# One sum of squares for two norms between the blocks of a fused fp32 transformer kernel

## The chip, the cores and the metric

The kernel runs on one core of one Trainium2 chip. The metric is the device time of one execution in microseconds (us), the median of the runs.

## What is computed

A sequence of 256 tokens of width 1024 passes through two blocks, all in fp32. The first block has two layers (mixed attention, cross attention to a memory, a gated MLP) and ends with a norm, the second block has two layers (retention, short convolution, each with a SwiGLU) and begins with another norm. Between the blocks the reference does this:

```python
def rms_norm(x, g):                        # end of the first block: g = norm_final
    y = x * lax.rsqrt(jnp.mean(x * x, axis=-1, keepdims=True) + EPS)
    return y * g

def rms_norm_2(x, gain=None):              # start of the second: gain = norm_mix_2[0]
    y = x * lax.rsqrt(jnp.mean(x * x, axis=-1, keepdims=True) + EPS)
    return y * gain

ax = modulate(rms_norm_2(hx, norm_mix[i]), sh1, sc1)     # hx = first block's output
ac = modulate(rms_norm_2(hc, norm_mix[i]), csh1, csc1)   # hc = the context
```

With x the residual stream and g the first norm's gain, the first norm gives y = x g r1, where r1 = 1 / sqrt(mean(x^2) + eps). The second norm's factor is r2 = 1 / sqrt(mean(y^2) + eps). The input of the retention is x g r1 r2 times the second gain, then scaled and shifted. Multiplied out, r1 r2 = 1 / sqrt(mean(x^2 g^2) + eps mean(x^2) + eps^2) = 1 / sqrt(mean(x^2 (g^2 + eps)) + eps^2). The residual stream of the second block is y, which needs r1 alone.

## The kernel before

Activations lie feature-first: 8 blocks (`kb`) of 128 features by 256 tokens. TensorE multiplies fp32 weights in split form: ScalarE copies each streamed piece of 128x1024 from the ring buffer to a high half `WH` (line 489), VectorE subtracts to get the low half `WL` (line 1067), and TensorE does high by high, high by low and low by high (`rows` or `FH`/`FL` hold the activations' halves). Two buffers each for `WH` and `WL` alternate. A piece can be split when TensorE is done with the piece two places before.

The weights stream through a ring of 8 pieces of 512 KB, issued by SyncE in one fixed order. SyncE issues a piece when VectorE has used the one 7 places before, and reports a piece as `loaded` only when it has issued the one 5 places behind it. So ScalarE can read a piece only when VectorE has used the piece three places ahead. Mixed into the stream are `ada` pieces, the modulation weights, which VectorE alone reduces (`ada_piece`, line 1084).

Each engine has its own program, in one fixed order; the order on an engine is that of the Python code of its block, and semaphores tie the engines together. A stage has steps of two pieces. Its loop takes `after(step)`, a function called behind every step, and so side work is set between pieces. The stages around the change are:

- `down` of layer 1 (k0 + 7, or K - 1): 11 steps, two pieces and two `ada` pieces a step. Its side work is the context's norm: ScalarE squares the context (steps 0 and 1), TensorE sums (`summed`), ScalarE copies the sums (`side_sums`), TensorE totals them (`total`), ScalarE takes the root (`raw_root`, behind a load of the table for square roots), VectorE takes the reciprocal (`root(rstd_m)`, line 1200), `scaled` (line 1206) on VectorE, `high` on ScalarE (line 621) and `low` (line 1233) on VectorE make the halves of the context's rows. Then the residual (line 1093) adds the sums in four banks to `x`.
- The gap between the blocks: squares of x, their sum, root, reciprocal (r1); squares of x times gain, their sum, times r1 squared, root, reciprocal (r2). Then eight times `scaled`, `high`, `low`, one for each block of features. `scr` has eight blocks of 128x256: `scr1` is its first half, for squares, `scr2` the second, for scaled blocks.
- `rq` (K), 4 steps: queries. `first_step` waits for each block's high and low. VectorE's side work at step 0 multiplies x by gain and r1 (line 1598); the rotations (`sine`, `turned_by`) begin at step 2.
- `rk` (K + 1), 4 steps with products over own and context rows, 512 columns wide, and two `ada` pieces a step; then `rg` (K + 2).

`turn_over` issues fill matmuls on zeros. `summed`, `gate_logits` and others sum into four groups of 32 rows of a bank, each with ones of 32 columns, to be totalled by a further matmul.

Of the kernel before, what the change touches and what calls it, by code (L numbers as in the profile page):

```python
# [7 lines left out]
S = 256  # L8
D = 1024
KB = D // 128  # L10
# [8 lines left out]
EPS = 1e-6  # L19
# [82 lines left out]
V_FINAL1 = _take(KB)  # L102
# [100 lines left out]
def transformer(nc, xT_d, memT_d, ctxT_d, cond_d, stream_d, vecs_d, const_d, rope1_d, rope2_d, decay_d,  # L203
                gw_d, w1_d, w2_d, out_d):
    F32, F32R, BF16 = mybir.dt.float32, mybir.dt.float32r, mybir.dt.bfloat16
    ALU, ACT, AX = mybir.AluOpType, mybir.ActivationFunctionType, mybir.AxisListType

    ctx = ExitStack()
    with ctx:  # L209
        def sb(name, shape, dt=F32):  # L210
            return ctx.enter_context(nc.sbuf_tensor(name, shape, dt))

        def sem(name):
            return ctx.enter_context(nc.semaphore(name))
# [6 lines left out]
        x = sb("x", [128, KB, S])  # L221
        both = sb("rows", [128, 2 * KB, 2, S + 2], F32R)
        AHs, ALs = both[:, 0:KB, :, :], both[:, KB:2 * KB, :, :]
        AH, AL = AHs[:, :, :, 0:S], ALs[:, :, :, 0:S]
        scr = sb("scr", [128, 8, S])
        scr1, scr2 = scr[:, 0:4, :], scr[:, 4:8, :]
        rms = sb("rms", [128, S])
# [33 lines left out]
        mod = sb("mod", [128, DEPTH * 48])  # L261
        modc = sb("modc", [128, 2 * KB])
        gs = sb("gs", [128, 6, KB])

        ARENA = 80 * 1024
        arena_at = nc.sbuf_base
# [2 lines left out]
        def at(name, shape, kb, dt=F32):  # L269
# [51 lines left out]
        misc = ob[1]  # L321
# [38 lines left out]
        in_cond, mod_ready, ret_sc, ret_w, ret_o, ret_g, ret_sq, ret_ms, ret_rms, ret_t, ret_h, ret_l = (  # L360
            sem(n) for n in ("in_cond", "mod_ready", "ret_sc", "ret_w", "ret_o", "ret_g", "ret_sq", "ret_ms", "ret_rms", "ret_t", "ret_h", "ret_l"))
        y_ready, out_done, ret_v = sem("y_ready"), sem("out_done"), sem("ret_v")
        both_ready = sem("both_ready")
        taken_ready = sem("taken_ready")
        tok_mm, tok_high, tok_low, ret_sum = (sem(n) for n in ("tok_mm", "tok_high", "tok_low", "ret_sum"))
        sum_ready, ms_done, gl_ready, gate_sum, conv_ready = (
            sem(n) for n in ("sum_ready", "ms_done", "gl_ready", "gate_sum", "conv_ready"))

# [113 lines left out]
        def _(act):  # L482
# [82 lines left out]
            def squares(blocks):  # L565

                def go():
                    act.preload_act_table(ACT.Sqrt)
                    for kb in range(KB):
                        x_is(n["x"] + kb // blocks + 1)  # L570
                        square(x, n["norm"], kb)
                return go
# [133 lines left out]
            for i in range(DEPTH):  # L706
# [172 lines left out]
                if i == 0:  # L879
                    raw_norm(k0 + 7, vecs[:, V_MIX + KB:V_MIX + 2 * KB], 0, 2, evac=last_rows)  # L880
                else:
                    def context(step):

                        if step in (0, 1):
                            act.wait_ge(in_ctx, 16)
                            for kb in range(4 * step, 4 * step + 4):
                                A(scr[:, kb, :], ctxT[:, kb, :], ACT.Square).then_inc(sq_ready, 1)
                        if step == 3:
                            side_sums()
                        if step == 5:  # L890
                            act.preload_act_table(ACT.Sqrt)
                            raw_root()
                        if step in (7, 9):
                            act.wait_ge(mod_ready, 1)
                            for kb in range(2 * step - 14, 2 * step - 10):
                                high(n["scaled"], kb, shift=modc[:, 0:8], sel=1)
                    weights(k0 + 7, last_rows, banks=False, tail=squares(2), after=context)
                    n["split"] += 1
                    n["scaled"] += 1
                    n["x"] += 4  # L900
# [22 lines left out]
                    n["x"] += 8  # L923


            def gained_square(kb):
                act.wait_ge(sq_used, 8 * n["norm"] + kb + 5)
                A(scr1[:, kb % 4, :], x[:, kb, :], ACT.Square, scale=vecs[:, V_FINAL1 + kb:V_FINAL1 + kb + 1]).then_inc(sq_ready, 1)
            for kb in range(4):
                gained_square(kb)  # L930
            act.wait_ge(sq_used, 8 * n["norm"] + 8)
            A(rms[:], misc[:, 0:S], ACT.Sqrt, bias=eps, scale=1.0 / D).then_inc(rms_ready, 1)
            for kb in range(4, KB):
                gained_square(kb)
            n["norm"] += 1
            act.wait_ge(both_ready, 1)
            A(rms[:], prod[:], ACT.Sqrt, bias=eps, scale=1.0 / D).then_inc(rms_ready, 1)
            n["norm"] += 1
            act.wait_ge(mod_ready, 1)
            for kb in range(KB):  # L940
                high(n["scaled"], kb, shift=mod_of(0, 0))
            n["split"] += 1
# [14 lines left out]
            def queries(i, s):  # L957
                A(Q2[:, i * 2 + s, :], proj[s][:, 0:S], ACT.Copy).then_inc(bank_free[s], 1)
                if s == 0 and i:
                    swap(i - 1)  # L960
            weights(K, queries, after=lambda step: None)

            def keys(i, s):
                A(K2[:, i * 2 + s, :], proj[s][:], ACT.Copy, scale=256 ** -0.5).then_inc(bank_free[s], 1)
# [95 lines left out]
        def _(dve):  # L1060
# [137 lines left out]
            def root(dst=None):  # L1198
                dve.wait_ge(rms_ready, n["norm"] + 1)
                chain.link(V.reciprocal((dst or rstd)[:], rms[:]))  # L1200
                n["norm"] += 1

            def scaled(m, src, gain, kb, by):
                if kb >= 4:
                    dve.wait_ge(nl_ready, 8 * m + kb - 3)
                V.scalar_tensor_tensor(out=scr2[:, kb % 4, :], in0=src[:, kb, :], scalar=gain[:, kb:kb + 1], in1=by[:],
                                       op0=ALU.mult, op1=ALU.mult).then_inc(t_ready, 1)
# [315 lines left out]
            def context_low(*blocks):  # L1523
                for kb in blocks:
                    low(n["split"], kb, sel=1, shift=modc[:, 0:8])

            def context(step):

                if step == 4:
                    chain.link(V.tensor_tensor(modc[:], modc[:], vecs[:, V_ADAB:V_ADAB + 16], ALU.add))  # L1530
                    modulations(0)
                    chain.link(V.tensor_tensor(gs[:, 5, :], gs[:, 0, :], vecs[:, V_FINAL1:V_FINAL1 + KB], ALU.mult))
                if step == 6:
                    root(rstd_m)
                    dve.wait_ge(in_ctx, 16)
                if step == 8:
                    context_low(0, 1, 2, 3)
                if step in (6, 8):
                    for kb in range(2 * step - 12, 2 * step - 8):
                        scaled(n["split"], ctxT, gs[:, 4, :], kb, rstd_m)  # L1540
            weights(K - 1, last_rows, into_x=True, after=context, ahead=lambda: context_low(4, 5, 6, 7))
            n["split"] += 1
            root()
            chain.link(V.tensor_tensor(rstd_m[:], rstd[:], rstd[:], ALU.mult))
            dve.wait_ge(sq_used, 8 * n["norm"] + 8)
            V.tensor_tensor(prod[:], ob[0][:, 0:S], rstd_m[:], ALU.mult).then_inc(both_ready, 1)
            root(rstd_m)
            chain.link(V.tensor_tensor(rstd_m[:], rstd_m[:], rstd[:], ALU.mult))
            for kb in range(KB):
                scaled(n["split"], x, gs[:, 5, :], kb, rstd_m)  # L1550
                if kb:
                    low(n["split"], kb - 1, shift=mod_of(0, 0))
            low(n["split"], KB - 1, shift=mod_of(0, 0))
# [39 lines left out]
            def turns(step):  # L1593

                if step == 0:
                    dve.wait_ge(in_rope2, 16)
                    for kb in range(KB):
                        V.scalar_tensor_tensor(out=x[:, kb, :], in0=x[:, kb, :], scalar=vecs[:, V_FINAL1 + kb:V_FINAL1 + kb + 1], in1=rstd[:],
                                               op0=ALU.mult, op1=ALU.mult).then_inc(x_ready, 1)
                    n["x"] += KB  # L1600
                if 3 <= step <= 10:
                    turned_by(step - 3)
                if 2 <= step <= 9:
                    sine(step - 2)
# [210 lines left out]
        def _(pe):  # L1815
# [3 lines left out]
            def mm(out, lhsT, rhs, start, stop):  # L1819
                return T.matmul(out, lhsT, rhs, start=start, stop=stop, skip_group_check=True)  # L1820

            def turn_over(count, bank=ob[0]):

                for _ in range(count):
                    mm(bank[:], still[:, 0:128], still[:], True, True)
# [7 lines left out]
            def sum_squares(kb, bank=misc):  # L1833
                pe.wait_ge(sq_ready, 8 * n["norm"] + kb + 1)
                mm(bank[:, 0:S], ones, scr1[:, kb % 4, :], kb == 0, kb == KB - 1).then_inc(sq_used, 1)
# [15 lines left out]
            def total():  # L1851

                pe.wait_ge(sum_ready, n["raw"] + 1)
                mm(misc[:, S:2 * S], ones, rms[:], True, True).then_inc(ms_done, 1)
                n["raw"] += 1
# [473 lines left out]
            def second_ffn(k, gated):  # L2329
                make(k, XS(AHs), XS(ALs), S + 2, raw=True)  # L2330
                add_gated(k + 1, gated - FB, FB)
            for bank in (misc, ob[0]):
                for kb in range(KB):
                    sum_squares(kb, bank)
                n["norm"] += 1
            n["split"] += 2
            turn_over(18, acc[3])

            def ret_scores(h):
                if h == 0:  # L2340
# [47 lines left out]
                pe.wait_ge(ret_qs, h + 1)  # L2388
                mm(proj[0][:, S:2 * S], ones, rms[:], True, True).then_inc(ret_ms, 1)

            make(K, X(AH), X(AL), fresh=True, after=lambda step: None)
            make(K + 1, XM(AH), XM(AL), 2 * S)
            make(K + 2, X(AH), X(AL), after=tokens)

# [156 lines left out]
```

## Time and profile before

| | before |
|---|---|
| median of 3 runs | 1561.16 us (1561.01 to 1561.27) |
| the profiled execution's own time | 1560.88 us |
| its span, first to last instruction | 1559.2 us |
| TensorE busy | 1530.3 us, 98% |
| VectorE busy | 1147.6 us, 74% |
| ScalarE busy | 865.2 us, 55% |
| GpSimd busy | 110.6 us, 7% |
| mean DMA rate | 191 GB/s |

The profile gives the time of every instruction in microseconds from the start of the span. PE is TensorE, PEld its weight loads, DVE VectorE, ACT ScalarE, POOL GpSimd, SP SyncE. A line number is that of the kernel, and it can be a helper's: every matmul has L1820. An fp32 matmul of the kind that isn't split appears as two records. The ends of matmuls are modelled and overlap the next start.

### The profile page before, as it was taken

How to read it: one execution, taken by the hardware profiler on the slowest of the kernel's cores; microseconds unless marked ns; L12 is line 12 of the kernel's file. 1: busy time of each engine (PE TensorE's matmuls, PEld its weight loads, DVE VectorE, ACT ScalarE, POOL GpSimd, SP SyncE). 2: the span in 40 equal slices, each digit the busy share in tenths (PEclk: the TensorE clock that was granted, in tenths of full speed). 3: DMA queues.
4: the chain of work that ended last, by engine and by line, in shares of the span. 5: the costliest groups of instructions: out<-in, count | busy, mean ns of one | idle time of the engine just before them, and what ended most of it. 6: DMA issues, size and time to landing. Idle time of an engine off the chain costs nothing. (4 is left out here: it accounts for less than half of the span.)

```text
span 1559.2 us, 35029 instructions
## 1 busy us (share of the span) xinstructions
PE 1530.3 (98%) x12576; PEld 1447.8 (93%) x12576; DVE 1147.6 (74%) x1707; ACT 865.2 (55%) x1444; POOL 110.6 (7%) x91
## 2 busy tenths in 40 slices
PE   9999999999999999999999999999999999999998
PEld 7977799999996879999888999999999999999997
DVE  6874788888876578888965556798887478676644
ACT  4665787754457578775543433346554365555533
POOL 2200012210300002220011000000000000000000
PEclk9999999999999999999999999999999999999999
DMA  9521455568641345558847534497888555455551
GB/s 373 198 82 54 150 166 185 188 213 272 244 163 55 122 156 187 183 189 303 292 136 224 167 126 171 148 344 257 278 272 265 185 166 178 160 189 186 179 188 41
DMA packets 84247, 297.62 MB, mean 191 GB/s; under 512 B 9664, under 2 KB 12480, under 8 KB 83392
## 3 DMA queue, kind: packets, MB, share of 16 engines
q1 hardware_dynamic: 78768, 283.24, 53.9%
q10 hardware_dynamic: 5392, 13.18, 2.5%
q8 instruction: 59, 0.97, 0.3%
q14 instruction: 28, 0.23, 0.0%
HBM read 291.40 MB, written 1.05 MB: 188 GB/s over the span
## 5 line engine op out<-in xcount | busy, mean ns | idle before, releaser
L489 ACT ACTIVATE WH<-ring 128x1024 fp32r<-128x1024 f32 (+1 forms) x418 | 441.3, 1058 | 502.5 <-PE projs L1820 256.5
L1067 DVE TENSOR_TENSOR WL<-ring,WH 128x1024 fp32r<-128x1024 f32 x427 | 524.4, 1229 | 224.4 <-ACT WH L489 222.8
L1820 PE MATMUL projs<-rows,WH 128*128 128x256 f32 (+2 forms) x3504 | 488.5, 288 | 1.8 <-ACT rows L621 0.7
L1820 PEld LDWEIGHTS projs<-rows,WH 128*128 128x128 f32 x3504 | 449.1, 189 | 15.1 <-issue 2.7
L1820 PE MATMUL projs<-rows,WL 128*128 128x256 f32 (+2 forms) x1808 | 260.6, 286 | 0.0
L1820 PEld LDWEIGHTS projs<-rows,WL 128*128 128x128 f32 x1808 | 235.6, 189 | 6.0 <-DVE WL L1067 2.1
L1820 PE MATMUL accs<-rows,WH 128*128 128x256 f32 (+2 forms) x1312 | 189.9, 283 | 3.7 <-DVE rows L1289 1.9
L1820 PE MATMUL accs<-FH,WH 128*128 128x256 f32 (+1 forms) x768 | 190.9, 284 | 1.2 <-DVE WL L1067 1.2
L1820 PE MATMUL accs<-FL,WH 128*128 128x256 f32 (+1 forms) x768 | 189.8, 281 | 0.0
L1820 PEld LDWEIGHTS accs<-rows,WH 128*128 128x128 f32 x1312 | 172.4, 189 | 7.3 <-DVE rows L1289 3.1
L1820 PEld LDWEIGHTS accs<-FH,WH 128*128 128x128 f32 x768 | 144.3, 188 | 3.1 <-issue 2.9
L1820 PEld LDWEIGHTS accs<-FL,WH 128*128 128x128 f32 x768 | 144.8, 189 | 0.0
L1084 DVE SCALAR_TENSOR_TENSOR ring<-ring,crow 128x1024 f32<-128x1024 f32 (+1 forms) x96 | 117.0, 1219 | 2.3
L1820 PE MATMUL accs<-FH,WL 128*128 128x256 f32 (+1 forms) x768 | 113.6, 282 | 0.9 <-DVE WL L1067 0.9
L1820 PE MATMUL accs<-rows,WL 128*128 128x256 f32 (+2 forms) x720 | 107.2, 283 | 0.0
L1820 PEld LDWEIGHTS accs<-FH,WL 128*128 128x128 f32 x768 | 101.1, 188 | 1.3 <-DVE WL L1067 1.3
L1820 PEld LDWEIGHTS accs<-rows,WL 128*128 128x128 f32 x720 | 94.7, 189 | 1.3 <-DVE WL L1067 0.7
L1795 POOL TENSOR_TENSOR FL<-prod,FH 128x256 f32 x44 | 62.5, 1422 | 330.5 <-ACT FH L553 330.5
L1462 DVE TENSOR_TENSOR cv<-cv,taps 128x510 f32<-128x510 f32 x44 | 30.4, 691 | 37.8 <-ACT cv L848 37.8
L848 ACT ACTIVATE cv<-mk,vecs 128x256 f32<-128x256 f32 x88 | 47.5, 588 | 0.0
L666 ACT ACTIVATE scr<-accs,nmax 128x256 f32<-128x256 f32 (+1 forms) x96 | 39.7, 435 | 8.7 <-DVE nmax L1261 8.7
L553 ACT ACTIVATE FH<-prod 128x256 fp32r<-128x256 f32 (+1 forms) x88 | 36.2, 411 | 9.6 <-DVE prod L1564 4.7
(284 smaller groups left out, 1727.4 us busy)
## 6 DMA issues: line engine op xcount, KB each, us to landing
ring<-in_stream SPq DMA_DIRECT2D x532, 512.0 KB, 4.2
W1v<-in_w ACTq DMA_DIRECT2D x2, 1024.0 KB, 7.8
W1k<-in_w ACTq DMA_DIRECT2D x2, 1024.0 KB, 11.6
D<-in_decay ACTq DMA_DIRECT2D x4, 512.0 KB, 5.3
x<-in_xT SPq DMA_DIRECT2D x2, 512.0 KB, 5.6
memT<-in_memT SPq DMA_DIRECT2D x1, 1024.0 KB, 10.0
mq<-P ACTq DMA_DIRECT2D x8, 128.0 KB, 6.1
ctxT<-in_ctxT ACTq DMA_DIRECT2D x1, 1024.0 KB, 8.2
```

What stands on the lines that cost most here:

```text
L489: A(WH[:, s, :], ring[:, r % RING, :], ACT.Copy).then_inc(wh_ready, 1)
L553: A(FH[:, step, :], prod[:], ACT.Copy).then_inc(fh_ready, 1)
L666: ins = A(prob[:, g, c:c + w], score[:, g, c:c + w], ACT.Exp, bias=nmax[:, u % 2, g, qt:qt + 1], accum_out=sums[:, u % 2, g, qt:qt + 1])
L848: ins = A(cv[:, s, :], us[:, s, :], ACT.Identity, bias=vecs[:, cb + j:cb + j + 1], scale=vecs[:, cw + 4 * FB + j:cw + 4 * FB + j + 1])
L1067: V.tensor_tensor(WL[:, s, :], ring[:, r % RING, :], WH[:, s, :].bitcast(F32), ALU.subtract).then_inc(consumed, 1)
L1084: V.scalar_tensor_tensor(out=piece, in0=piece, scalar=1.0, in1=crow[:], op0=ALU.mult, op1=ALU.mult, accum_out=mod[:, bass.ds(j, 1)]).then_ ...
L1462: chain.link(V.tensor_tensor(cv[:, :, 1:S], cv[:, :, 1:S], taps[:, :, 0:S - 1], ALU.add))
L1795: G.tensor_tensor(FL[:, bass.ds(step, 1), :].squeeze(1), prod[:], FH[:, bass.ds(step, 1), :].squeeze(1).bitcast(F32), ALU.subtract).then_i ...
L1820: return T.matmul(out, lhsT, rhs, start=start, stop=stop, skip_group_check=True)
```

## The change

The squares of x are taken once, into all eight blocks of `scr` (`block_squares`), as the tail of `down`. TensorE sums them twice: with columns of g^2 + eps (`g2eps`) as the stationary operand, broadcast to 128 columns, which gives the sum of x^2 (g^2 + eps) over all features; and with ones of 32 columns into four groups of rows of `ob[0]`. The first sum, with eps^2 as the bias, gives the product of both factors by one root and one reciprocal, and `scaled` uses it. The second sum is copied by ScalarE after step 0 of `rq`, totalled by TensorE after step 1, its root taken after step 2, its reciprocal after step 3, and x is multiplied by gain and r1 after step 0 of `rk`. The fill matmuls in the gap go from 18 to 8. Three small VectorE operations make `g2eps` and eps^2. In `down`, the context's side work from ScalarE's `side_sums` on moves one step earlier; TensorE's part of it stays where it is, and so do VectorE's last four lows. The load of the table for square roots ahead of the squares is gone.

```diff
@@ tiles, semaphores
+        g2eps = sb("g2eps", [128, KB])
+        eps2 = sb("eps2", [128, KB])
-        both_ready = sem("both_ready")
+        own_mm = sem("own_mm")
@@ ScalarE, down of layer 1
-                        if step == 3:
+                        if step == 2:
                             side_sums()
-                        if step == 5:
+                        if step == 4:
                             act.preload_act_table(ACT.Sqrt)
                             raw_root()
-                        if step in (7, 9):
+                        if step in (6, 8):
                             act.wait_ge(mod_ready, 1)
-                            for kb in range(2 * step - 14, 2 * step - 10):
+                            for kb in range(2 * step - 12, 2 * step - 8):
                                 high(n["scaled"], kb, shift=modc[:, 0:8], sel=1)
-                    weights(k0 + 7, last_rows, banks=False, tail=squares(2), after=context)
+                    def block_squares():
+                        for kb in range(KB):
+                            x_is(n["x"] + kb // 2 + 1)
+                            A(scr[:, kb, :], x[:, kb, :], ACT.Square).then_inc(sq_ready, 1)
+                    weights(k0 + 7, last_rows, banks=False, tail=block_squares, after=context)
@@ ScalarE, between the blocks
-            def gained_square(kb):
-                act.wait_ge(sq_used, 8 * n["norm"] + kb + 5)
-                A(scr1[:, kb % 4, :], x[:, kb, :], ACT.Square, scale=vecs[:, V_FINAL1 + kb:V_FINAL1 + kb + 1]).then_inc(sq_ready, 1)
-            for kb in range(4):
-                gained_square(kb)
+            act.wait_ge(mod_ready, 1)
             act.wait_ge(sq_used, 8 * n["norm"] + 8)
-            A(rms[:], misc[:, 0:S], ACT.Sqrt, bias=eps, scale=1.0 / D).then_inc(rms_ready, 1)
-            for kb in range(4, KB):
-                gained_square(kb)
+            A(rms[:], misc[:, 0:S], ACT.Sqrt, bias=eps2[:, 0:1], scale=1.0 / D).then_inc(rms_ready, 1)
             n["norm"] += 1
-            act.wait_ge(both_ready, 1)
-            A(rms[:], prod[:], ACT.Sqrt, bias=eps, scale=1.0 / D).then_inc(rms_ready, 1)
-            n["norm"] += 1
-            act.wait_ge(mod_ready, 1)
...
-            weights(K, queries, after=lambda step: None)
+            def own_norm(step):
+                if step == 0:
+                    act.wait_ge(own_mm, 1)
+                    A(rms[:], ob[0][:, 0:S], ACT.Copy).then_inc(sum_ready, 1)
+                if step == 2:
+                    raw_root()
+            weights(K, queries, after=own_norm)
@@ VectorE, down of layer 1
-                if step == 4:
+                if step == 3:
+                    first_gain = vecs[:, V_FINAL1:V_FINAL1 + KB]
+                    chain.link(V.tensor_tensor(g2eps[:], first_gain, first_gain, ALU.mult))
+                    chain.link(V.tensor_scalar(g2eps[:], g2eps[:], EPS, None, ALU.add))
+                    chain.link(V.tensor_tensor(eps2[:, 0:1], eps, eps, ALU.mult))
...
-                if step == 6:
+                if step == 5:
                     root(rstd_m)
                     dve.wait_ge(in_ctx, 16)
-                if step == 8:
+                if step == 7:
                     context_low(0, 1, 2, 3)
-                if step in (6, 8):
-                    for kb in range(2 * step - 12, 2 * step - 8):
+                if step in (5, 7):
+                    for kb in range(2 * step - 10, 2 * step - 6):
                         scaled(n["split"], ctxT, gs[:, 4, :], kb, rstd_m)
-            weights(K - 1, last_rows, into_x=True, after=context, ahead=lambda: context_low(4, 5, 6, 7))
+                if step == 9:
+                    context_low(4, 5, 6, 7)
+            weights(K - 1, last_rows, into_x=True, after=context)
@@ VectorE, between the blocks
             root()
-            chain.link(V.tensor_tensor(rstd_m[:], rstd[:], rstd[:], ALU.mult))
-            dve.wait_ge(sq_used, 8 * n["norm"] + 8)
-            V.tensor_tensor(prod[:], ob[0][:, 0:S], rstd_m[:], ALU.mult).then_inc(both_ready, 1)
-            root(rstd_m)
-            chain.link(V.tensor_tensor(rstd_m[:], rstd_m[:], rstd[:], ALU.mult))
+            dve.wait_ge(own_mm, 1)
             for kb in range(KB):
-                scaled(n["split"], x, gs[:, 5, :], kb, rstd_m)
+                scaled(n["split"], x, gs[:, 5, :], kb, rstd)
@@ VectorE, turns
+                if step == 3:
+                    root(rstd_m)
+                if step == 4:
                     for kb in range(KB):
                         V.scalar_tensor_tensor(out=x[:, kb, :], in0=x[:, kb, :], scalar=vecs[:, V_FINAL1 + kb:V_FINAL1 + kb + 1], in1=rstd_m[:],
@@ TensorE
-            for bank in (misc, ob[0]):
-                for kb in range(KB):
-                    sum_squares(kb, bank)
-                n["norm"] += 1
+            pe.wait_ge(mod_ready, 1)
+            for kb in range(KB):
+                pe.wait_ge(sq_ready, 8 * n["norm"] + kb + 1)
+                mm(misc[:, 0:S], g2eps[:, kb:kb + 1].to_broadcast([128, 128]), scr[:, kb, :], kb == 0, kb == KB - 1).then_inc(sq_used, 1)
+            for kb in range(KB):
+                c = kb % 4
+                ins = mm(ob[0][32 * c:32 * c + 32, 0:S], ones[:, 0:32], scr[:, kb, :], kb < 4, kb >= 4)
+            ins.then_inc(own_mm, 1)
+            n["norm"] += 1
             n["split"] += 2
-            turn_over(18, acc[3])
+            turn_over(8, acc[3])
...
-            make(K, X(AH), X(AL), fresh=True, after=lambda step: None)
+            make(K, X(AH), X(AL), fresh=True, after=lambda step: total() if step == 1 else None)
```

## Rows read from the trace of the kernel before

**Rows 1.** The page, busy us, share of the span, instructions, by engine.

```profile
PE 1530.3 (98%) x12576; PEld 1447.8 (93%) x12576; DVE 1147.6 (74%) x1707; ACT 865.2 (55%) x1444; POOL 110.6 (7%) x91
```

**Rows 2.** TensorE's waits, 736 to 770: us in total, times, longest.

```profile
PE accs L1820 <- DVE WL L1067: 2.1, 3, 1.2
```

**Rows 3.** VectorE's timeline in `down`: start, us, instruction, [idle before <-releaser].

```profile
745.39 1.22 DVE L1067 TENSOR_TENSOR WL<-ring,WH 128x1024 fp32r<-128x1024 f32 x1 [0.51 <-ACT WH L489]
...
747.67 1.75 DVE L1200 RECIPROCAL rstd_m<-rms 128x256 f32<-128x256 f32 x1
...
751.05 1.22 DVE L1067 TENSOR_TENSOR WL<-ring,WH 128x1024 fp32r<-128x1024 f32 x1
...
760.17 1.66 DVE L1233 SCALAR_TENSOR_TENSOR rows<-scr,modc,rows 128x256 fp32r<-128x256 f32 x4
...
767.90 1.67 DVE L1233 SCALAR_TENSOR_TENSOR rows<-scr,modc,rows 128x256 fp32r<-128x256 f32 x4
769.49 2.47 DVE L1093 TENSOR_TENSOR x<-x,accs 128x512 f32<-128x512 f32 x4
```

**Rows 4.** TensorE's timeline in `down`: low passes, and the last piece's start.

```profile
731.20 1.12 PE L1820 MATMUL accs<-FH,WL 128*128 128x256 f32 x8
...
734.50 1.12 PE L1820 MATMUL accs<-FH,WL 128*128 128x256 f32 x8
...
746.02 1.12 PE L1820 MATMUL accs<-FH,WL 128*128 128x256 f32 x8
...
748.90 1.12 PE L1820 MATMUL accs<-FH,WL 128*128 128x256 f32 x8
...
752.32 1.22 PE L1820 MATMUL accs<-FH,WL 128*128 128x256 f32 x8 [0.39 <-DVE WL L1067]
...
766.98 0.36 PE L1820 MATMUL accs<-FH,WH 128*128 128x256 f32 x1 [1.16 <-DVE WL L1067]
```

**Rows 5.** ScalarE's timeline in `down`: the piece behind step 4.

```profile
735.65 1.06 ACT L489 ACTIVATE WH<-ring 128x1024 fp32r<-128x1024 f32 x1 [2.24 <-PE accs L1820]
```

**Rows 6.** TensorE's timeline between the blocks.

```profile
770.67 3.72 PE L1820 MATMUL ob<-scr,const 128*128 128x256 f32 x16 [0.58 <-ACT scr L563]
...
778.36 4.05 PE L1820 MATMUL accs<-still 128*128 128x512 bf16 x18
783.11 6.35 PE L1820 MATMUL projs<-rows,WH 128*128 128x256 f32 x32 [0.70 <-ACT rows L621]
...
791.91 2.12 PE L1820 MATMUL projs<-rows,WH 128*128 128x256 f32 x16 [0.57 <-ACT Q L958]
```

**Rows 7.** VectorE's timeline between the blocks.

```profile
774.15 1.22 DVE L1067 TENSOR_TENSOR WL<-ring,WH 128x1024 fp32r<-128x1024 f32 x1 [0.94 <-ACT WH L489]
776.11 1.75 DVE L1200 RECIPROCAL rstd<-rms 128x256 f32<-128x256 f32 x1 [0.73 <-ACT rms L932]
...
781.88 0.88 DVE L1206 SCALAR_TENSOR_TENSOR scr<-x,gs,rstd_m 128x256 f32<-128x256 f32 x2
```

**Rows 8.** Timeline of the kernel's last norm, TensorE and VectorE.

```profile
1546.67 3.69 PE L1820 MATMUL ob<-scr,const 128*128 128x256 f32 x16 [0.15 <-PE accs L1820]
...
1551.03 1.75 DVE L1200 RECIPROCAL rstd<-rms 128x256 f32<-128x256 f32 x1 [3.41 <-ACT rms L576]
1552.82 3.26 DVE L1241 SCALAR_TENSOR_TENSOR ybuf<-x,vecs,rstd 128x256 f32<-128x256 f32 x8
```

**Rows 9.** TensorE's timeline, eight sums of 32 columns in a later stage.

```profile
1261.69 1.07 PE L1820 MATMUL ob<-scr,const 128*32 128x256 f32 x16
```

**Rows 10.** VectorE's timeline in `rq`: x times gain and rstd.

```profile
793.90 3.25 DVE L1598 SCALAR_TENSOR_TENSOR x<-x,vecs,rstd 128x256 f32<-128x256 f32 x8
```

**Rows 11.** TensorE's timeline, the kernel's first matmuls.

```profile
1.39 7.01 PE L1820 MATMUL ob<-still 128*128 128x512 bf16 x18 [1.39 <-POOL still L1738]
```

**Rows 12.** Windows: stretch, its us, busy us by engine, granted clock, DMA share.

```profile
769.50:783.10 13.60, 12.15 (x55) 7.85 (x55) 10.66 (x15) 8.58 (x21) 0.00 (x0) 1.00 0.42 148
783.10:791.90 8.80, 7.92 (x48) 6.21 (x49) 5.99 (x15) 4.78 (x10) 0.00 (x0) 1.00 0.00 0
```

More of the change, by code:

```diff
@@ L1527, in context @@
             def context(step):
-                if step == 4:
+                if step == 3:
[3 more added lines that the diff above has]
+                    chain.link(V.tensor_tensor(eps2[:, 0:1], eps, eps, ALU.mult))
                     chain.link(V.tensor_tensor(modc[:], modc[:], vecs[:, V_ADAB:V_ADAB + 16], ALU.add))
                     modulations(0)
-                    chain.link(V.tensor_tensor(gs[:, 5, :], gs[:, 0, :], vecs[:, V_FINAL1:V_FINAL1 + KB], ALU.mult))
-                if step == 6:
+                    chain.link(V.tensor_tensor(gs[:, 5, :], gs[:, 0, :], first_gain, ALU.mult))
+                if step == 5:
                     root(rstd_m)
                     dve.wait_ge(in_ctx, 16)
-                if step == 8:
+                if step == 7:
                     context_low(0, 1, 2, 3)
-                if step in (6, 8):
-                    for kb in range(2 * step - 12, 2 * step - 8):
+                if step in (5, 7):
+                    for kb in range(2 * step - 10, 2 * step - 6):
                         scaled(n["split"], ctxT, gs[:, 4, :], kb, rstd_m)
-            weights(K - 1, last_rows, into_x=True, after=context, ahead=lambda: context_low(4, 5, 6, 7))
+                if step == 9:
+                    context_low(4, 5, 6, 7)
+            weights(K - 1, last_rows, into_x=True, after=context)
             n["split"] += 1
             root()
-            chain.link(V.tensor_tensor(rstd_m[:], rstd[:], rstd[:], ALU.mult))
-            dve.wait_ge(sq_used, 8 * n["norm"] + 8)
-            V.tensor_tensor(prod[:], ob[0][:, 0:S], rstd_m[:], ALU.mult).then_inc(both_ready, 1)
-            root(rstd_m)
-            chain.link(V.tensor_tensor(rstd_m[:], rstd_m[:], rstd[:], ALU.mult))
+            dve.wait_ge(own_mm, 1)
             for kb in range(KB):
-                scaled(n["split"], x, gs[:, 5, :], kb, rstd_m)
+                scaled(n["split"], x, gs[:, 5, :], kb, rstd)
                 if kb:
@@ L1596, in turns @@
                     dve.wait_ge(in_rope2, 16)
+                if step == 3:
+                    root(rstd_m)
+                if step == 4:
                     for kb in range(KB):
-                        V.scalar_tensor_tensor(out=x[:, kb, :], in0=x[:, kb, :], scalar=vecs[:, V_FINAL1 + kb:V_FINAL1 + kb + 1], in1=rstd[:],
+                        V.scalar_tensor_tensor(out=x[:, kb, :], in0=x[:, kb, :], scalar=vecs[:, V_FINAL1 + kb:V_FINAL1 + kb + 1], in1=rstd_m[:],
                                                op0=ALU.mult, op1=ALU.mult).then_inc(x_ready, 1)
```

## The prediction

> **What bounds the kernel now.** I read the page first. TensorE is busy for 98% of the span [rows 1], so time can only be won where TensorE waits or does work that can go. Next I read TensorE's waits inside the stage ahead of the change, then the timelines of the three engines around the boundary between the blocks.
>
> In `down` of layer 1, the last stage of the first block, TensorE waits three times for VectorE's low halves `WL`, 2.1 us in all [rows 2]. VectorE's timeline says why: its split `WL` at 745.39 still has 0.51 us of idle before it (so has the one before it), and from 747.67 it never rests until the residual at 769.49 [rows 3]. The context's reciprocal and scalings lie there on top of two splits and two `ada` pieces a step. TensorE's low passes come every 2.88 us, as 748.90 after 746.02, but 752.32 is 3.42 after 748.90, and the last piece starts at 766.98 after 1.16 us of idle [rows 4].
>
> Then comes the gap between the blocks. TensorE starts the first sum of squares at 770.67, the first product of `rq` at 783.11 and its second step at 791.91 [rows 6]. The chain is: first sum (TensorE) to 774.4, ScalarE's root, reciprocal at 776.11, a product of rstd with itself, a product with the second sum, a second root, a second reciprocal, one more product, and the first `scaled` at 781.88 [rows 7]. After that, eight pairs of `scaled` and `low` on VectorE set the pace. The 18 fill matmuls end at 782.4, ahead of the product, so they don't bind [rows 6].
>
> **The change part by part.** All times below are in the clock of the profile before, unless I say "shifted".
>
> *(a) One root and one reciprocal in place of two.* The new chain (sum, root, reciprocal, scaling) is the one that the kernel runs as its last norm, so I price it from there: sum starts 1546.67, reciprocal 1551.03 (4.36 later), first scaling 1552.82 (6.15 later) [rows 8]. From 770.67 this gives the reciprocal at 775.03 and the first `scaled` at 776.82. VectorE must be free: its second split for `rq` ran from 774.15 to 775.37 [rows 7], behind ScalarE's second `WH`, which stands behind the squares. The squares now need no freed buffer (eight buffers instead of four), so they follow the residual, which ends some 2.5 us after 769.49, plus two squares; that is 0.3 to 0.4 us earlier than now. The split then ends at about 775.0, just in time. First `scaled` at 776.84 instead of 781.88: **5.0 us** less; 4.7 if the split isn't earlier. Gone with it are four gained squares and four VectorE products, all inside this difference.
>
> *(b) The first sum has another stationary operand*, a column of `g2eps` broadcast, in place of ones. Same eight fp32 matmuls, 3.72 us [rows 6]. I take zero; the pace of that group is the bound, and a stride can't make a loading of 128 columns shorter.
>
> *(c) The own sums, eight matmuls to four groups of 32 rows.* The same form takes 1.07 us for its 16 records [rows 9]. They end at about 775.3; VectorE waits for them (`own_mm`) before its first `scaled`, which overwrites their input, and would start only at 776.84. Hidden, with 1.5 us to spare. The Trainium skill (TensorEngine Tiling, Key Properties) says that a change of tiling mode drains TensorE, which speaks against inserting these here. With the drain the own sums would end a little later; as they have 1.5 us to spare, the result by that rule is the same unless a drain costs more than this. The 1.07 us group lies between products of full width [rows 9].
>
> *(d) Eight fill matmuls instead of 18.* 18 take 4.05 us [rows 6], so eight take 1.8: 775.3 to 777.1. The first product comes 1.23 us after the first `scaled` (783.11 after 781.88), so at 778.07. Not binding. TensorE idles 0.95 us there, against 0.70 now.
>
> *(e) The pairs* keep their number and form; the stretch from first `scaled` to 791.91 moves as a whole. Its end is ScalarE's `WH` and `Q`, which depend on TensorE alone.
>
> *(f) The first norm's own root.* The total is one more fp32 matmul of full width on TensorE, after step 1 of `rq`, where TensorE is never idle, so it is paid in full. In `down` the same total makes the low passes 731.20 and 734.50 lie 3.30 apart instead of 2.88 [rows 4]: **0.4 us** more. ScalarE's copy and root (under 0.5 us each) lie in its idle time: a piece costs it a `WH` (1.06 us [rows 5]) and a short copy, against 2.8 us or more of TensorE. VectorE's reciprocal, 1.75 us [rows 7], comes after step 3, where VectorE has two splits of 1.2 us a step, and the eight scalings of x, 3.25 us [rows 10], move from step 0 of `rq` to step 0 of `rk`. There a step has 512 columns, and a piece lasts twice as long; a split made late by 3.3 us is for a piece that TensorE begins some 5.6 us later. Zero, both before (the split behind the scalings stalled nothing) and after. Queued behind this ScalarE and VectorE work are only splits and the rotations, whose DMAs have many us.
>
> *(g) The context's steps, each one earlier in `down`.* Three more small VectorE operations at step 3 (0.6 us together, like the five there now) meet no late piece. ScalarE's table load and root after step 4 fall into 2.24 us of idle ahead of the `WH` at 735.65 [rows 5]; TensorE's total, between its low passes 731.20 and 734.50, is done in time. The reciprocal and four scalings, 3.38 us (747.67 to 751.05), now begin at 741.9. The four lows and four scalings, twice 1.6 us from 760.17, come one step earlier too [rows 3]. The last lows stay directly ahead of the residual. VectorE's work is the same; what it gains is the idle in front of its splits of step 6, twice 0.51 us. Followed piece by piece: the root's block ends at 745.3, TensorE waits 0.55 for the low half wanted at 746.02, VectorE catches up to within a piece, the second block makes it wait 0.7 near 758.2, the last piece's low half is ready at 765.7, when TensorE is just through with the one before, and the 1.16 us of idle is gone. The lows end at 768.4, and the residual starts 1.0 to 1.1 us earlier. ScalarE may read a ring entry only when VectorE has used the entry three places ahead; with these times that comes before the need each time. **1.0 us** less, between nothing and 1.2.
>
> Sum: 5.0 + 1.0 - 0.4 = 5.6 us. Behind the gap TensorE waits for nothing that hangs on an absolute time: before the second step of `rq` the ring is full (no DMA runs from 783.1 to 791.9 [rows 12]), and a shorter pause leaves it full. So the gain reaches the end whole. Against the profiled execution's own time of 1560.88 us (span 1559.2) this gives 1555.3; the median of the runs is 0.28 us above that execution, so the forecast is **1555.5 us**.
>
> **The rivals.**
>
> *A. The earlier context steps win nothing.* VectorE is late by a whole block at steps 6 and 8 instead of 7 and 9; if these make ScalarE's `WH` wait for ring entries, VectorE idles later for what it saved. For it: many `WH` here start on a release by the ring. Against: every block is absorbed within two pieces. Time 1555.5 + 1.0 = 1556.5 us.
>
> *B. The own sums become the wait.* If the four row groups don't overlap, eight matmuls take as long as the first sum, 3.7 us instead of 1.1, and end near 777.9; `scaled` starts 1.1 us late, and the fills end at 779.7, 0.5 us after the product then could start. Time 1555.5 + 1.6 = 1557.1 us. Against: [rows 9].
>
> *C. TensorE's clock falls, and the kernel is slower.* Ten fills are gone and its idle there is longer. Fills at the start of the kernel took 7.01 us for 18 against 4.05 here, near the ratio of 1.2 to 2.4 GHz [rows 6, 11]. At the low clock, a pair's four products take 0.94 us instead of 0.47 and exceed VectorE's 0.79: 1.2 us over eight; the 16 low products cost 1.9 more, each further piece 2.8. With one further piece at half clock the gain is gone (3.1 + 2.8 = 5.9); with two it is 8.7, and the kernel ends at 1564.2 us, slower than before. Against: the granted clock is 1.00 through this gap with 1.45 us unused of 13.6 [rows 12], and the idle on either side of the fills grows by only a quarter of a us. The Trainium skill (TensorE: Matmul & The Clock Gate, What's actually happening) has the clock follow recent activity, which is why I keep this rival; by that rule, too, it would need a much longer idle than here, I judge.
>
> **How the numbers follow.** My forecast (1555.0 to 1556.1) 0.70; A 0.10; B 0.07; A and B or another small wait, to 1558, 0.06; a gain that some wait eats to under 0.2% 0.03; C 0.04. About 0.2%, 3.1 us, is what a measurement of this kernel can tell from no change. All but the last two cases lie beyond it: faster 0.93, same 0.03, slower 0.04. For the range I take the bounds of the terms: 5.1 + 1.2 - 0.4 = 5.9 at best, with a little for squares that start TensorE sooner, 1554.8; at worst A or B, 1557.2.
>
> **What the profile will show.** (a) One reciprocal in the gap, some 4.4 us after the first sum starts, and the first `scaled` 6.2 us after it. (c) `ob<-scr` of 128x32 form, 1.1 us, done before the reciprocal ends. (d) Fills ended before the first product, clock 1.00. (f) One `ob<-rms` matmul in `rq` that puts its low passes 0.4 us further apart, and no waits for `WL` from there on. (g) VectorE without idle from 741.9, the residual near 768.4, TensorE's waits for `WL` 1.0 us less in all. I am wrong if `scaled` starts later than 7 us after the first sum, if the residual isn't earlier, or if TensorE waits again in `rq` or `rk`.

## The result: 8.6 us faster, 5.6 forecast

The changed kernel takes 1552.56 us (1552.5 to 1552.7, 5 runs), the kernel before 1561.16 us beside it. The ratio is 0.9944, with a 95% interval of 0.9934 to 0.9954. The sign is the one forecast; the time lies 2.2 us below the stated range. The profiled execution took 1552.56 us, its span 1550.9 us, 8.3 us less than before.

The page of the changed kernel, busy time by engine, against [rows 1]:

```profile
PE 1519.6 (98%) x12554; PEld 1441.3 (93%) x12568; DVE 1148.5 (74%) x1707; ACT 862.3 (56%) x1436; POOL 111.7 (7%) x91
```

TensorE's waits for `WL` from 736 to 770 (us in total, times, longest), and its timeline around the gap, both of the changed kernel:

```profile
PE accs L1830 <- DVE WL L1072: 1.2, 2, 0.8
```

```profile
736.39 1.11 PE L1830 MATMUL accs<-FH,WL 128*128 128x256 f32 x8
739.23 1.11 PE L1830 MATMUL accs<-FH,WL 128*128 128x256 f32 x8
...
745.57 1.21 PE L1830 MATMUL accs<-FH,WL 128*128 128x256 f32 x8 [0.47 <-DVE WL L1072]
...
757.86 1.21 PE L1830 MATMUL accs<-FH,WL 128*128 128x256 f32 x8 [0.76 <-DVE WL L1072]
...
768.57 3.69 PE L1830 MATMUL ob<-scr,g2eps 128*128 128x256 f32 x16 [0.69 <-ACT scr L903]
772.19 1.07 PE L1830 MATMUL ob<-scr,const 128*32 128x256 f32 x16
773.42 1.67 PE L1830 MATMUL accs<-still 128*128 128x512 bf16 x7 [0.16 <-issue]
775.83 6.35 PE L1830 MATMUL projs<-rows,WH 128*128 128x256 f32 x32 [0.73 <-ACT rows L623]
782.02 2.04 PE L1830 MATMUL projs<-rows,WL 128*128 128x256 f32 x16
784.63 2.12 PE L1830 MATMUL projs<-rows,WH 128*128 128x256 f32 x16 [0.58 <-ACT Q L955]
786.59 1.11 PE L1830 MATMUL projs<-rows,WL 128*128 128x256 f32 x8
...
789.42 1.11 PE L1830 MATMUL projs<-rows,WL 128*128 128x256 f32 x8
790.37 0.59 PE L1830 MATMUL ob<-rms,const 128*128 128x256 f32 x2
...
792.68 1.11 PE L1830 MATMUL projs<-rows,WL 128*128 128x256 f32 x8
```

VectorE's timeline of the changed kernel:

```profile
739.77 1.22 DVE L1089 SCALAR_TENSOR_TENSOR ring<-ring,crow 128x1024 f32<-128x1024 f32 x1
740.92 0.09 DVE L1089 DVE_READ_ACCUMULATOR ring<-ring,crow 128x1 f32 x1
740.92 1.75 DVE L1205 RECIPROCAL rstd_m<-rms 128x256 f32<-128x256 f32 x1
...
767.28 2.48 DVE L1098 TENSOR_TENSOR x<-x,accs 128x512 f32<-128x512 f32 x4
...
771.56 1.23 DVE L1072 TENSOR_TENSOR WL<-ring,WH 128x1024 fp32r<-128x1024 f32 x1 [0.53 <-ACT WH L491]
772.87 1.75 DVE L1205 RECIPROCAL rstd<-rms 128x256 f32<-128x256 f32 x1
774.66 0.88 DVE L1211 SCALAR_TENSOR_TENSOR scr<-x,gs,rstd 128x256 f32<-128x256 f32 x2
...
816.86 3.25 DVE L1608 SCALAR_TENSOR_TENSOR x<-x,vecs,rstd_m 128x256 f32<-128x256 f32 x8
```

From the first sum to the first product it is now 7.26 us, before 12.44 [rows 6]: 5.2 us less. The residual starts 2.2 us earlier than in [rows 3], where 1.0 to 1.1 were forecast. The total puts its low passes 3.26 us apart (789.42 to 792.68) where neighbours there lie 2.83 apart (786.59 to 789.42): 0.4 us more. So everything around the change was about as forecast, except the residual. The rest of the gain is elsewhere. Windows in stages that the change doesn't touch show it: `down` of layer 0 (340 to 370) and the second block's first `f2` (1200 to 1235). Columns: stretch, its us, TensorE's busy us and matmuls, granted clock, DMA share, GB/s. The kernel before:

```profile
340.00:370.00 30.00, 30.00 (x252) 1.00 0.85 277
1200.00:1235.00 35.00, 35.00 (x294) 1.00 0.57 185
```

The changed kernel:

```profile
340.00:370.00 30.00, 30.00 (x255) 1.00 0.85 280
1200.00:1235.00 35.00, 35.00 (x297) 1.00 0.57 184
```

TensorE is busy without a break in both, at the same granted clock and DMA share, and gets through 1% more matmuls. The same shows in low passes 2.84 us apart (736.39 to 739.23), before 2.88 [rows 4]. It occurs where matmuls read `FH` and `FL`; a stage that reads `rows` instead, the 960 products ahead of the last `f2`, takes 115.20 us in both kernels. Landmarks from the chains of both traces (start, us, engine and line, instructions) tell how the lead grows behind the gap. The kernel before:

```profile
1193.13 63.60 PE accs L1820 x528
...
1367.73 115.20 PE projs L1820 x960
```

The changed kernel, start of the same stage, the 960 products, and the start of the last norm's sums:

```profile
1186.28 59.81 PE accs L1830 x504
...
1360.04 115.20 PE projs L1830 x960
...
1538.34 3.71 PE ob L1830 x16
```

The lead is 6.85 us at 1186.28, where the second block's first `f2` begins, and 8.33 at the last norm (1546.67 in [rows 8]): 1.5 us won behind 1186.28, by work that the change doesn't touch.

### The profile page after: what moved, and what is told of

Its sections match the earlier page's. It is cut to its first block and busy times, and to the rows that moved or that the text cites. A ratio compares the mean times of both kernels' runs of the same rounds, so it can differ in the third digit from the quotient of the medians.

```text
span 1550.9 us, 34990 instructions
## 1 busy us (share of the span) xinstructions
PE 1519.6 (98%) x12554; PEld 1441.3 (93%) x12568; DVE 1148.5 (74%) x1707; ACT 862.3 (56%) x1436; POOL 111.7 (7%) x91
```

## The experiments

**Whose are the extra 2.8 us?** The change declares two tiles, `g2eps` and `eps2`, 64 bytes per partition together, ahead of the arena that holds `FH` and `FL`. My theory (P): the place of what lies in the arena sets the pace. The rival (S): something in the stream of instructions does. First the kernel before with nothing but a gap:

```diff
         gs = sb("gs", [128, 6, KB])
+        sb("gap", [128, 2 * KB])
```

> The kernel before, with an unused tile of 64 bytes per partition put where the change puts its two new tiles, so that all that lies in the arena (FH, FL and the rest) starts 64 bytes later; nothing else is touched. Theory P (placement): the unforeseen 2.8 us of the change are a shorter low-pass pitch (2.88 to about 2.85 us) in the stages that read FH and FL, and come from where these lie. Then this kernel takes about 1558.3 us. Rival S (the stream of instructions or something else in the change sets the pace): 1561.2 us, no change.

Measured: 1558.52 us, before 1561.23; ratio 0.9981, interval 0.9972 to 0.999. The windows of this kernel:

```profile
340.00:370.00 30.00, 30.00 (x255) 1.00 0.85 277
1200.00:1235.00 35.00, 35.00 (x298) 1.00 0.58 190
```

64 unused bytes give 2.7 us and the pace of the changed kernel, with the program otherwise as before. P holds, S falls. The reverse, the changed kernel with its arena where it was:

```diff
-        g2eps = sb("g2eps", [128, KB])
-        eps2 = sb("eps2", [128, KB])
...
         sb("arena", [128, ARENA // 4])
+        g2eps = sb("g2eps", [128, KB])
+        eps2 = sb("eps2", [128, KB])
```

> The changed kernel, with its two new tiles put behind the arena, so that the arena lies where it lay before the change. Theory P: about 1555.4 us (1552.6 + 2.8), and low passes in the first layer's down stage 2.88 us apart. Rival S: 1552.6 us, as the changed kernel.

Measured: 1555.34 us (1554.94 to 1555.4) against 1561.23; ratio 0.996, interval 0.9946 to 0.9973. Its windows are back at 252 and 294 matmuls:

```profile
340.00:370.00 30.00, 30.00 (x252) 1.00 0.85 275
1200.00:1235.00 35.00, 35.00 (x294) 1.00 0.56 184
```

The landmarks of this kernel, and its fills in the gap (for (c) below):

```profile
774.14 1.90 PE L1830 MATMUL accs<-still 128*128 128x512 bf16 x8
...
1187.20 63.59 PE accs L1830 x528
...
1540.73 3.71 PE ob L1830 x16
```

Its lead over the kernel before is 5.93 us at the first `f2` and 5.94 at the last norm: with the arena in its old place nothing is won between them.

Without the shift the change is worth 1561.23 - 1555.34 = 5.9 us, where 5.6 were forecast. The shift itself is worth 1555.34 - 1552.56 = 2.8 us by the medians, 2.4 by the profiled executions (1554.94 and 1552.56): 0.9 in the two `down` stages, for in this kernel the residual starts at 768.22, in the changed one at 767.28, and the rest, 1.4, behind them. The changed kernel's 1552.56 is from the earlier measurement; the kernel before took 1561.16 beside it and 1561.23 beside these runs.

**What are the context's earlier steps worth?** Once added to the kernel before, once taken out of the changed kernel (the same lines the other way round):

```diff
-                        if step == 3:
+                        if step == 2:
                             side_sums()
-                        if step == 5:
+                        if step == 4:
...
-                if step == 6:
+                if step == 5:
                     root(rstd_m)
```

> The kernel before, with only the context's side work in down of layer 1 moved one step earlier. My prediction's step (g): the residual starts 1.0 to 1.1 us earlier, 1560.1 us. Rival A: no gain, 1561.2 us.

> The changed kernel, with the context's side work back where it was before the change. If step (g) is worth 1.0 us there: 1553.6 us. Rival A: 1552.6 us. If the earlier steps were also what sped up down's pieces (a rival to placement), more than 1.5 us is lost: over 1554.1 us.

Measured: 1560.0 us against 1561.23 (ratio 0.9991, interval 0.9982 to 1.0), 1.2 us less; the interval reaches 1, so the ratio alone doesn't settle it; but none of its 11 runs took more than 1560.17 and none of the 21 beside them less than 1561.0, and the traces agree. The other way 1553.91 us (1553.01 to 1554.85), 1.4 us above the changed kernel. VectorE's timeline of the first of these two kernels:

```profile
741.87 1.75 DVE L1200 RECIPROCAL rstd_m<-rms 128x256 f32<-128x256 f32 x1
...
768.24 2.48 DVE L1093 TENSOR_TENSOR x<-x,accs 128x512 f32<-128x512 f32 x4
```

This kernel has no shift of the arena. Its residual comes 1.25 us earlier than in [rows 3]; TensorE's waits for `WL` in 736 to 770 fall from 2.1 us [rows 2] to 0.9:

```profile
PE accs L1820 <- DVE WL L1067: 0.9, 2, 0.5
```

Rival A (no gain) falls. The second kernel's residual starts at 768.24, against 767.28 in the changed one. It keeps the changed kernel's pace, with 255 and 297 matmuls in the two windows, so the earlier steps are not what sped these stages up.

**Which place?** The kernel before with other gaps ahead of the arena (`[128, KB]` for 32 bytes, `3 * KB`, `4 * KB`), and with the 64 byte gap ahead of `WH` or behind `WX` instead.

> The kernel before, with an unused tile of 32 bytes per partition ahead of the arena: the arena then starts at a multiple of 128 bytes (before it starts 96 past one, after the change 32 past one). If the pitch of the FH passes is set by how their operands lie against lines of 64 or 128 bytes, this aligned place is at least as fast as the one after the change: 1558.5 us or less. If only the 64 byte step matters otherwise: 1561.2 us.

> The kernel before, with an unused tile of 128 bytes per partition ahead of the arena: the arena again starts 96 past a multiple of 128. If the place modulo 128 decides: 1561.2 us. If the distance to other tiles or a coarser position decides: something else, 1558.5 us if every shift helps.

> The kernel before, with an unused tile of 96 bytes per partition ahead of the arena, which then starts 64 past a multiple of 128. By lines of 64 bytes: as the 32 byte gap. By lines of 128 bytes: between the 32 byte gap and before.

> The kernel before, with an unused tile of 64 bytes per partition ahead of WH, so that WH, WL, rows, scr and all behind them move together with the arena. If the arena's own place decides: 1558.5 us, but for what the other tiles' new places do. If the distance between the arena and the weights' halves decides: 1561.2 us.

> The kernel before, with the 64 byte gap between WX and x: the weights' halves WH, WL and WX stay, and all behind them, the arena too, moves by 64 bytes. If the distance between the weights' halves and the FH and FL that they are multiplied with decides: as with the gap ahead of the arena, about 1558.4 us, 297 or 298 matmuls in 1200 to 1235 instead of 294. If the arena's distance to a tile between x and gs decides: 1561.0 us and 294.

| gap, where | median us (range), before beside it | ratio, 95% interval | matmuls in 340 to 370, 1200 to 1235 |
|---|---|---|---|
| none | 1561.16 | | 252, 294 |
| 32, arena | 1559.9 (1559.76 to 1561.0), 1561.0 | 0.9995, 0.9985 to 1.0004 | 256, 294 |
| 64, arena | 1558.52 (1558.34 to 1559.53), 1561.23 | 0.9981, 0.9972 to 0.999 | 255, 298 |
| 96, arena | 1555.9 (1553.58 to 1557.55), 1561.0 | 0.9963, 0.995 to 0.9975 | 257, 300 |
| 128, arena | 1557.77 (1557.44 to 1558.78), 1561.0 | 0.9981, 0.9972 to 0.9991 | 256, 298 |
| 64, ahead of WH | 1561.16 (1560.95 to 1562.15), 1561.0 | 1.0002, 0.9992 to 1.0011 | 252, 294 |
| 64, behind WX | 1559.23 (1558.06 to 1559.82), 1561.13 | 0.9985, 0.9976 to 0.9994 | 252, 301 |

The aligned place (32 bytes on, where the arena starts at a multiple of 128) is one of the slower ones: its gain is not clear of the noise, as its interval reaches over 1. And 128 bytes on, the same place modulo 128, isn't the old one; nor is the fastest place, 96 bytes on, what either rule would give. So alignment to lines of 64 or 128 bytes is not the cause. With the gap ahead of `WH` the arena lies at the same address as with the gap ahead of the arena, and nothing is won: it is not the arena's address alone that counts, but how it lies to something that moves with `WH`. With the gap behind `WX` the `f2` stage is fast and `down` of layer 0 is not, so the two don't hang on one distance alone. The last three kernels ran once each:

> The kernel with the 64 byte gap ahead of the arena, but FH set 64 bytes back, to where it lay before; so against the kernel before FL moves by 64 bytes (with the rest of the arena) and FH does not. If FL's place decides: 255 matmuls in 340 to 370 and 298 in 1200 to 1235, as with the gap. If FH's place decides: 252 and 294, as before.

```diff
-        FH = at("FH", [128, FB, S], 0, F32R)
+        FH = at("FH", [128, FB, S], -0.0625, F32R)
```

> The kernel before with the 64 byte gap ahead of crow, so that crow, mod, modc and gs move with the arena. Only the stages with ada pieces read crow. If crow's distance to the arena decides in layer 0's down: 252 in 340 to 370, and 298 in 1200 to 1235, where nothing reads crow. If crow has no part: 255 and 298.

> The kernel before with the 64 byte gap ahead of scr, so that x and rows stay and scr, vecs, const and all behind them move with the arena. Where this agrees with the gap ahead of the arena (255, 298), tiles between scr and the arena have no part; where it agrees with the gap behind WX (252, 301), x and rows have none.

| | one time, us (before beside it 1560.94) | matmuls in 340 to 370, 1200 to 1235 |
|---|---|---|
| FL moved, FH not | 1557.85 | 256, 298 |
| gap ahead of crow | 1559.29 | 255, 297 |
| gap ahead of scr | 1557.7 | 258, 297 |

The kernel with the gap ahead of the arena ranges over 1.2 us by itself, so these single times rank nothing; the counts are what I go by. `FL`'s place is enough: its windows are those of the gap to within one matmul, though `FH` lies where it lay before. Whether `FH`'s place alone would do too was not run. `crow` has no part. `scr` and what stands behind it have none in `f2`. The partner of `FL` stays open. If it is one tile, `f2` says that it lies from `WH` to `WX`, which stay in place when the gap stands behind them and move when it stands ahead; but the 301 matmuls with the gap behind `WX`, against 297 or 298 with the gap further back, say that `x` or `rows` has some part too. For `down` of layer 0 I can't say even that much: without an effect behind `WX` and with one ahead of `scr`, `x` or `rows` would have to matter, which it doesn't read; and the count there has a scatter of its own, for the changed kernel without fills, below, shows 258 with the placement of the changed kernel, which has 255.

**Does the gain of placement add up?** The changed kernel with 32 more bytes ahead of the arena:

```diff
         eps2 = sb("eps2", [128, KB])
+        sb("gap", [128, KB])
```

> The changed kernel with another 32 bytes ahead of the arena, so that it lies 96 bytes further than before the change, the place that gave the kernel before its largest gain. If that gain adds to the change's steps: 2 to 2.5 us below the changed kernel, about 1550.3 us. If the changed kernel's other differences undo it: 1552.6 us.

Measured: 1549.81 us (1549.04 to 1550.88); ratio 0.9931, interval 0.9917 to 0.9944. It beats both kernels, the changed one (measured earlier) by 2.75 us. Its windows:

```profile
340.00:370.00 30.00, 30.00 (x267) 1.00 0.88 296
1200.00:1235.00 35.00, 35.00 (x300) 1.00 0.59 190
```

And the start of its first sum:

```profile
765.93 3.69 PE L1831 MATMUL ob<-scr,g2eps 128*128 128x256 f32 x16 [0.80 <-ACT scr L904]
```

In `f2` that is the 300 of the 96 byte gap, as it should be. In `down` of layer 0 it is 267, and the 96 byte gap, with every tile at the same place, has 257. So placement doesn't fix the pace of that stage; what else does stays open. Most of the gain lies ahead of the gap between the blocks, in the two `down` stages: the first sum starts 2.6 us ahead of the changed kernel's (768.57), out of 3.5 us in all by the profiled executions (1552.56 and 1549.04). The median came out as forecast, but not by `f2`'s pace alone, and the 96 byte gap's own runs, from 1553.58 to 1557.55, are spread the widest of all.

**The fills and the clock.** The changed kernel with 18 fills, `turn_over(18, acc[3])`, and with that line left out:

> The changed kernel with 18 fill matmuls in the gap instead of 8. They end near 777.4, where the first product started at 775.8. Prediction's step (d), read the other way: the product waits, 1.3 to 1.7 us later at its start; but VectorE's pairs set the pace, so part of it is caught up in the pairs: 1552.8 to 1554.2 us. If fills cost nothing: 1552.6 us.

> The changed kernel without any fill matmuls in the gap: TensorE has nothing to do for about 2.6 us ahead of the first product. Rival C (the clock falls when TensorE idles there): a granted clock under 1.00 after the gap and at least 3 us more, over 1555 us. Against it: 1552.6 us, as with 8.

Measured: 1552.75 us (1552.66 to 1552.92) and 1552.35 us (1551.99 to 1552.78), both some 0.2 us from the changed kernel. TensorE's timeline with 18 fills:

```profile
768.66 3.69 PE L1830 MATMUL ob<-scr,g2eps 128*128 128x256 f32 x16 [0.73 <-ACT scr L903]
...
776.99 5.28 PE L1830 MATMUL projs<-rows,WH 128*128 128x256 f32 x32
...
782.11 2.04 PE L1830 MATMUL projs<-rows,WL 128*128 128x256 f32 x16
```

And without any:

```profile
767.98 3.69 PE L1830 MATMUL ob<-scr,g2eps 128*128 128x256 f32 x16 [0.71 <-ACT scr L903]
...
775.23 6.36 PE L1830 MATMUL projs<-rows,WH 128*128 128x256 f32 x32 [2.56 <-ACT rows L623]
781.43 2.06 PE L1830 MATMUL projs<-rows,WL 128*128 128x256 f32 x16
```

From the first sum to the 16 low products it is 13.45 us in both, as in the changed kernel (768.57 to 782.02). The 18 fills hold the first product back by 1.1 us, where I expected 1.3 to 1.7, and all of it is caught up in the pairs, because VectorE sets their pace and TensorE has room between them. So the fills cost nothing that these runs can tell. Without fills the granted clock does fall; the windows of that kernel (columns as in [rows 12]):

```profile
766.00:772.00 6.00, 5.29 (x35) 4.31 (x38) 5.45 (x8) 3.74 (x10) 0.00 (x0) 1.00 0.83 321
772.00:782.00 10.00, 7.37 (x53) 6.30 (x42) 8.53 (x18) 4.21 (x9) 0.00 (x0) 0.83 0.30 100
777.00:779.00 2.00, 2.00 (x12) 2.00 (x11) 2.00 (x6) 1.36 (x3) 0.00 (x0) 0.50 0.00 0
780.00:782.00 2.00, 2.00 (x16) 1.79 (x15) 0.84 (x2) 0.51 (x1) 0.00 (x0) 1.00 0.00 0
```

The mean is 0.83 from 772 to 782, which holds the 2.56 us of idle ahead of the first product (775.23) and the pairs behind it. From 777 to 779 it is 0.50, the lower level (1.2 of 2.4 GHz), and from 780 on full speed again. It costs nothing here, as the slow stretch lies in the paced pairs. The mechanism of rival C is real, its price isn't: I had it last through the low products and two further pieces. I had also judged that it would need a much longer idle than in this gap; 2.56 us, against 0.73 with eight fills, was enough. With eight fills it doesn't occur, by the windows of the changed kernel:

```profile
767.20:775.80 8.60, 7.05 (x45) 4.55 (x46) 7.74 (x11) 4.62 (x12) 0.00 (x0) 1.00 0.84 301
775.80:784.60 8.80, 7.92 (x48) 6.21 (x48) 5.99 (x15) 4.79 (x10) 0.00 (x0) 1.00 0.03 10
```

The Trainium skill (TensorE: Matmul & The Clock Gate, What's actually happening), by which activity holds the clock up, agrees with these windows.

## Why the prediction was wrong, point by point

The step that failed is the one under the sum that takes the rest of the kernel as unchanged ("So the gain reaches the end whole"): in the sum there is no term for the stages that read `FH` and `FL`, and two new tiles, 64 bytes together, were put at nothing without a reason. That missing term is 2.8 us (1555.34 - 1552.56), more than the width of the range, 2.4. Without the shift the same change takes 1555.34 us, inside the range and 0.2 from the forecast. The sum term by term, with the context's steps by the kernels without the shift:

| step | forecast us | shown us |
|---|---|---|
| (a) to (e) the gap, first sum to first product | -5.0 | -5.2 (12.44 to 7.26) |
| (e) pairs, first product to second step of rq | 0 | 0 (8.80 in both) |
| (f) total in rq | +0.4 | +0.4 |
| (g) context's steps | -1.0 | -1.25 (residual at 768.24 or 768.22, from 769.49) |
| residual to first sum | 0 | +0.1 (1.29, from 1.18) |
| placement of the arena | none | -2.8 |
| in all | -5.6 | -8.6 (the terms as rounded here add up to -8.75) |

(a) was right in form: one reciprocal, 4.3 us after the first sum, and the first `scaled` 6.1 us after it, as in the last norm. The second split did run just ahead of the reciprocal (771.56 to 772.8). (b) The broadcast column costs nothing: 3.69 us for the sums, against 3.72. (c) The own sums took 1.07 us and were over 1.4 us before `scaled`; rival B is refuted. No idle shows on either side of them: they start as the first sum ends, and the 0.16 us behind them in the changed kernel stands where the first of eight fills has no record; in the kernel with the arena in its old place, where all eight have one, the sums start at 773.14 and the fills at 774.14. (d) Eight fills don't bind. With 18 they hold the first product back, but the stage is no longer for it; with none it is no shorter. (f) The scalings of x at 816.86 made no product wait; TensorE has no new wait for `WL` in `rq` or `rk`. (g) The piece by piece account was right: waits of 0.47 and 0.76 us where 0.55 and 0.7 were forecast, and the last one gone. Its size was 0.2 us short, though the root began where I put it (741.87). The idle of 0.51 us ahead of a split is counted from the end of the 0.08 us read of the accumulator behind each `ada` product, and work that is ready starts beside that read: in the changed kernel the product of 739.77 has its read at 740.92, and the reciprocal starts at 740.92 too. So each of the two gaps was worth 0.59 us, 1.2 in all.

The low end of the range, 1554.8, was made only of the terms that I had named, so it could not hold this one. Nor could the signs of being wrong warn of it: `scaled` started 6.1 us after the first sum, the residual was earlier, and no wait came in `rq` or `rk`. All three are about the stages around the change, and a third of the gain came from the place of the tiles.

## What to carry to other kernels

When an edit declares or resizes a tile, everything behind it in memory moves, and a kernel that TensorE bounds to 98% can change its pace by 1 to 2% in whole stages (294 to 301 matmuls in the same 35 us here): put a new tile behind the others to measure an edit by itself, and try a few gaps of 32 bytes as a tuning of their own, which gave 2.75 us on top here. To tell placement from the edit, count the matmuls in a window of an untouched stage in both traces, in more than one such stage: one here moved by itself (257 and 267 with every tile in the same place). A serial chain (sum, root, reciprocal, scale) is priced well from another place where the same kernel runs it; and side work on an engine that is late is best moved to where that engine still idles, even if it lands on the same stage.

## What the runs showed of the hardware that was not expected

- The pace of fp32 products with the same shapes, clock and operands depends on where a moving operand lies against other tiles: 294 to 301 matmuls in 35 us of one stage, with shifts of 32 to 128 bytes of the arena or of what stands ahead of it. A common shift of all tiles from `WH` on changed nothing (294).
- Alignment to 128 bytes did not help: 294 in `f2` with the arena on a multiple of 128, 300 with it 64 past one.
- With every tile at the same place, one stage (`down` of layer 0) still ran at two paces in two kernels, 257 and 267 matmuls in the same 30 us. What sets them apart is not known.
- With 2.56 us of idle between the sums and the first product, the granted clock was 0.50 from 777 to 779 and 1.00 again from 780; with eight fills in the idle it was 1.00 from 767.2 to 784.6.
